# Two of the four weight sums of a pair on GpSimd in block 0, w_out pieces split ahead of the work on h, and a buffer of its own for the first pair

## The chip, the cores and the metric

The kernel runs on one core of a Trainium2 chip. The metric is the time on the device in microseconds (us), the median of several executions.

## The reference, cut to what matters

One layer of a streaming encoder for 2048 prompt frames (x_prompt) and 64 frames of a running stream (x_sample), model width 1024:

```
h = rmsnorm(x) * g_mix
q, f, i, g = split(h @ w_in)               # HGRN2: 8 heads of 128
o = chunked gated recurrence(q, f, i)      # chunks of 64 frames
x = x + (rmsnorm(o) * silu(g)) @ w_out
gate, up = split((rmsnorm(x) * g_ffn) @ w_gu)   # width 2816 each
x = x + (silu(gate) * up) @ w_down
```

Results are also the states of both streams; caches of the layers that this depth does not reach are copied.

## The kernel before, in words

**Blocks.** Frames lie in the free dimension. Block 0 has 576 columns (512 prompt frames and the 64 sample frames, T0), blocks 1 to 3 have 512 (TB). Block 0 is unrolled apart, since `first(b)` is true for it alone; blocks 1 to 3 are one loop. Each block runs through: 8 heads (w_in products with the recurrence of the head before between them), w_out, gate-up with w_gu, and down with w_down, in three groups of 6, 8 and 8 of the 22 gate-up pairs (`GROUPS`), each group followed by its share of down.

**Precision.** Nearly every float32 product is done as three products of split parts: `hi` is a copy rounded to fp32r (ScalarE), `lo` is the rest (VectorE, a subtraction), and TensorE adds hi*hi, hi*lo and lo*hi. So each weight piece of 128x512 costs one ScalarE copy and one VectorE subtraction before TensorE may use it. w_in, w_out and w_down pieces go through a ring of four slots (`w_raw`, `w_hi`, `w_lo`, `LEAD` = 3): L731 is the copy, L910 the subtraction.

**Gate-up.** A pair j is one step of Strassen's method (Winograd's form) over the halves of the 128 gate and 128 up outputs and the two halves of the frames: seven products (`A11, S2, S3, S1, A22, A12, S4`, in this order) of 12 matmuls each (L518 to L520). A11, A12, A22 are raw loads (`g_raw`), S1 to S4 are sums of raw parts (`g_x`): S1 = A21 + A22, S2 = S1 - A11, S3 = A11 - A21, S4 = A12 - S2. In block 0 VectorE makes all four (`weight_sum`, L1121, L1126, L1129, L1134) and SyncE stores S3, S4 and the split parts of S1 and S2 in HBM (`keep`); blocks 1 to 3 load these (`load_kept`). There is one buffer for each operand: while pair j is multiplied, pair j+1 is summed, copied (ScalarE, `gu_high`, L791) and subtracted (VectorE, `gu_low`, L1138), and the raw parts of pair j+2 are loaded as each buffer comes free (`load_first`, `keep`): A21 and A11 once S3 of pair j+1 is summed, then the stores of S3 and, after the subtraction of S1, four stores of S1 and S2, then A22 once its subtraction is done, then S4's store, then A12. All of these are issued by SyncE in this order.

The products are evicted from five banks of PSUM: ScalarE copies A11's to `p1u3` (L817), VectorE adds S2's (`u2`, L1175), S3's (`p1u3`, L1181), and S1's and A22's into `ebuf[:, 0]` (the gate add, L1187), multiplies by the norm `xrstd` (L1192), ScalarE copies A12's (L826), VectorE adds S4's (L1196). S4's product uses A22's bank, so TensorE starts it after the gate add. SiLU (L795), the product with up (L1146), and its split (L799, L1151) give the operand of down.

**Around w_out.** `p1u3` and `u2` are the two halves of `ebuf[:, 1]`, which also holds squares of x for the norm: ScalarE squares a tile into `ebuf[:, 0]` or `[:, 1]` (L615), GpSimd adds it to `ssq` (L1316, eight adds a norm), TensorE sums over partitions with `ones` (`norm_sum`, L291), and ScalarE takes the root (`norm`, L600 to L606). The first pair of a block therefore waits with its first copy (L817) for all eight adds; `norm_sum` stands after the first pair's S4 on TensorE, `norm` behind the copy of A12. `output_group` works off two x tiles at a time: residual add (L1070), scaling (L753), sums and splits of h2 (L1078 to L1095), and between them splits of the next w_out pieces. In blocks 1 to 3 three w_out pieces (6, 7, 8) are split ahead of that work, and piece 9 stands at the end of the first group.

**Last head.** For each head the squares of its output (L643) are split (L651, L988) and summed over partitions (L362, L363), and rstd, scale, y and y's split follow (L657 to L972); TensorE runs products of w_out for the first seven heads in between.

Of the kernel before, what the change touches and what calls it, by code (L numbers as in the profile page):

```python
# [19 lines left out]
P = 128  # L20
EPS = 1e-6
D = 1024
KT = D // P
# [40 lines left out]
def hybrid_layer(nc, x_t, w_all, gain_mix, gain_ffn, bounds, out_gain, state_in, y_t, state_p, state_s,  # L64
# [52 lines left out]
    a_lo, a_end = place("a_lo", [P, GT, T0], F32R)  # L117
    g_at = at[0]
# [148 lines left out]
    p1u3, u2 = ebuf[:, 1, 0:TH0], ebuf[:, 1, TH0:T0]  # L267
# [15 lines left out]
    with nc.Block() as block:  # L283

        @block.tensor
        def _(pe):
# [73 lines left out]
            def out_square_sum(b, h):  # L360
                pe.wait_ge(osq_lo_ready, HEADS * b + h + 1)
                pe.matmul(ps_s[:, 0:TB], ones_r[:], osq_hi[:, 0:TB], start=True, stop=False)  # L362
                mm = pe.matmul(ps_s[:, 0:TB], ones_r[:], osq_lo[:, 0:TB], start=False, stop=True)  # L363
                if first(b):
                    pe.matmul(ps_k[:, 0:CH], ones_r[:], osq_hi[:, TB:T0], start=True, stop=False)
                    mm = pe.matmul(ps_k[:, 0:CH], ones_r[:], osq_lo[:, TB:T0], start=False, stop=True)
                mm.then_inc(oms_done, 1)
# [155 lines left out]
            def gate_up(b, T, j, after_out=False, after_down=None):  # L523

                J = FT * b + j
                if after_out:
# [12 lines left out]
                    for o in (S2, S3, S1, A22, A12):  # L539
                        strassen(b, T, o, KH - 1, KH).then_inc(g_done, 1)  # L540
                    operand_ready(b, j, S4)
                    bank_free(J, S4)
                    strassen(b, T, S4, 0, KH).then_inc(g_done, 1)
                    norm_sum(b, T, 2 * b + 1)
# [53 lines left out]
        def _(act):  # L598
# [41 lines left out]
            def out_squares(b, h):  # L640
# [9 lines left out]
                act.wait_ge(osq_ready, HEADS * b + h + 1)  # L650
                nc.scalar.activation(osq_hi[:, 0:T], osq[:, 0:T], ACT.Copy).then_inc(osq_hi_ready, 1)  # L651
# [149 lines left out]
            def gate_up(b, T, j, j0, more, begun=True, norm_at=None, after_down=None):  # L801

                J, n = FT * b + j, T // 2
                nxt = [o for o in split_of(b)] if more else []
# [10 lines left out]
                if isinstance(j, int) and j == 0:  # L815
                    act.wait_ge(ssq_ready, (KT + 1) * (2 * b + 2))
# [4 lines left out]
                high(S3, S1, A22)  # L821
                act.wait_ge(g_done, OPERANDS * J + A12 + 1)
# [4 lines left out]
                if norm_at is not None:  # L827
                    norm(b, T, norm_at)
# [18 lines left out]
            def block_program(b, T):  # L847
# [57 lines left out]
        def _(dve):  # L905
# [79 lines left out]
            def low_squares(b, h):  # L985
                T = T0 if first(b) else TB
                dve.wait_ge(osq_hi_ready, HEADS * b + h + 1)
                nc.vector.tensor_tensor(osq_lo[:, 0:T], osq[:, 0:T], osq_hi[:, 0:T].bitcast(F32),  # L988
# [109 lines left out]
            def output_group(b, T, i):  # L1098

                def next_piece(u):  # L1100
                    if (i > 0 or u == 3 or first(b)) and (i < KT // 2 - 1 or u == 0):
                        output_pieces(b, i + (u + 3) // 4, (u + 3) % 4, (u + 3) % 4 + 1)
# [13 lines left out]
            def weight_sum(j, o):  # L1116
                if o == S1:
                    dve.wait_ge(g_loaded[RAW_A21], 16 * (j + 1))
                    dve.wait_ge(g_loaded[RAW_A22], 16 * (j + 1))
                    wait(dve, g_lo_ready, OPERANDS * j)  # L1120
                    nc.vector.tensor_tensor(g_x[:, 0], g_raw[:, RAW_A21], g_raw[:, RAW_A22], ALU.add).then_inc(g_sum_ready, 1)  # L1121
                elif o == S2:
                    dve.wait_ge(g_loaded[RAW_A11], 16 * (j + 1))
                    dve.wait_ge(g_sum_ready, 4 * j + 1)
                    wait(dve, g_sum_stored[1], 16 * j)
                    nc.vector.tensor_tensor(g_x[:, 1], g_x[:, 0], g_raw[:, RAW_A11], ALU.subtract).then_inc(g_sum_ready, 1)  # L1126
                elif o == S3:
# [26 lines left out]
            def gate_up(b, T, j, j0, more, begun=True):  # L1154

                J, n = FT * b + j, T // 2
                nxt = list(split_of(b)) if more else []
# [14 lines left out]
                total(S1, S2)  # L1172
# [21 lines left out]
                total(S4)  # L1194
# [4 lines left out]
            def down(b, T, f):  # L1199
                ahead = split_of(b) if f + 1 < len(GROUPS) else ()  # L1200
                last = f + 1 == len(GROUPS)
                for m in range(KT):
# [3 lines left out]
                    if m < len(ahead):  # L1206
                        j1 = GROUPS[f + 1][0]
                        if first(b) and m == 0:
                            for o in (S1, S2, S3):
                                weight_sum(j1, o)  # L1210
# [15 lines left out]
            def block_program(b, T):  # L1226
# [78 lines left out]
        def _(pool):  # L1305
            def sum_squares(nth, T):
# [33 lines left out]
            def block_program(b, T):  # L1340
# [12 lines left out]
                sum_squares(2 * b + 1, T)  # L1353
# [32 lines left out]
        def _(sp):  # L1386
# [98 lines left out]
            def block_program(b, T):  # L1485
# [12 lines left out]
                else:  # L1498
                    sp.wait_ge(y_lo_ready, HEADS * (b + 1))
                    for part in range(3):  # L1500
                        load_kept(b, 0, 0, part)
                        q = OUT0 + (2 + part) * RING
                        load_pieces(b, q, q + RING)
                col = 0 if first(b) else T0 + TB * (b - 1)
                nxt = T0 + TB * b
                for f, (j0, n) in enumerate(GROUPS):
                    with sp.Fori(j0 + 1, j0 + n) as j:
# [3 lines left out]
                    if f < len(GROUPS) - 1:  # L1511
                        load_pieces(b, DN0 + P_GROUP * f + RING, DN0 + P_GROUP * (f + 1) + RING)
# [123 lines left out]
```

## Time and profile before

| | us |
|---|---|
| median of 3 runs | 2716.09 (2714.62 to 2722.4) |
| the profiled execution's own time | 2717.68 |
| its span | 2716.0 |
| TensorE matmul busy | 2607.2 (96%) |
| VectorE busy | 1808.4 (67%) |
| ScalarE busy | 1274.7 (47%) |
| GpSimd busy | 276.2 (10%) |
| mean granted TensorE clock | 0.987 of full |

Engines in the rows: PE is TensorE's matmul, PEld its weight load, DVE VectorE, ACT ScalarE, POOL GpSimd, SP SyncE. "idle before" is the time an engine stood idle ahead of a group of instructions, and "<-" names what ended it. Block 0 takes the first 800 us or so, each other block some 636 us.

### The profile page before, as it was taken

How to read it: one execution, taken by the hardware profiler on the slowest of the kernel's cores; microseconds unless marked ns; L12 is line 12 of the kernel's file. 1: busy time of each engine (PE TensorE's matmuls, PEld its weight loads, DVE VectorE, ACT ScalarE, POOL GpSimd, SP SyncE). 2: the span in 40 equal slices, each digit the busy share in tenths (PEclk: the TensorE clock that was granted, in tenths of full speed). 3: DMA queues.
4: the chain of work that ended last, by engine and by line, in shares of the span. 5: the costliest groups of instructions: out<-in, count | busy, mean ns of one | idle time of the engine just before them, and what ended most of it. 6: DMA issues, size and time to landing. Idle time of an engine off the chain costs nothing.

```text
span 2716.0 us, 53926 instructions
## 1 busy us (share of the span) xinstructions
PE 2607.2 (96%) x16804; PEld 2386.9 (88%) x16804; DVE 1808.4 (67%) x3187; ACT 1274.7 (47%) x2319; POOL 276.2 (10%) x197
## 2 busy tenths in 40 slices
PE   8999979999899999999999999899999999899998
PEld 7999879899898887999997888799898888699897
DVE  6666777876756667676665666767565667767665
ACT  5555543433435555443345555534344555544343
POOL 3111110000011112000002111200002111200001
PEclk9999989999999999999999999999999999999999
DMA  5212335644542223656653222557465222366564
GB/s 183 93 59 62 113 125 165 205 151 143 189 143 71 80 71 105 202 185 194 190 169 107 74 70 82 167 182 240 144 186 160 71 70 74 114 213 211 167 217 147
DMA packets 203414, 379.70 MB, mean 140 GB/s; under 512 B 23168, under 2 KB 23200, under 8 KB 203056
## 3 DMA queue, kind: packets, MB, share of 16 engines
q1 hardware_dynamic: 202896, 369.73, 43.2%
q0 software_dynamic: 384, 8.44, 0.9%
q8 instruction: 53, 0.87, 0.1%
q14 instruction: 81, 0.66, 0.1%
HBM read 331.67 MB, written 52.74 MB: 142 GB/s over the span
## 4 chain that ended last, share of the span: by engine, by line
PE 64%; DVE 4%; issue 3%; ACT 2%; DMA 1%; POOL 1%; SPq 1%; DVEq 0%; ACTq 0%; POOLq 0%
PE ps L426 11%; PE ps L428 11%; PE ps L427 11%; PE ps L518 7%; PE ps L519 7%; PE ps L520 7%; PE ps_s L518 1%; PE ps_s L520 1%; PE ps_s L519 1%; PE ps_u L336 1%; PE ps_s L315 1%; PE ps_o L349 1%; PE ps_u L337 1%; PE ps_o L351 1%; ACT h_raw L753 1%
## 5 line engine op out<-in xcount | busy, mean ns | idle before, releaser
L518 PE MATMUL ps<-h,g_hi 128*128 128x256 f32 (+1 forms) x2112 | 614.7, 291 | 60.1 <-DVE ebuf L1187 34.5
L519 PE MATMUL ps<-h,g_hi 128*128 128x256 f32 (+1 forms) x2112 | 608.9, 288 | 0.0
L520 PE MATMUL ps<-h,g_lo 128*128 128x256 f32 (+1 forms) x2112 | 608.6, 288 | 0.0
L910 DVE TENSOR_TENSOR w_lo<-w_raw,w_hi 128x512 fp32r<-128x512 f32 x512 | 374.5, 733 | 244.9 <-ACT w_hi L731 244.7
L426 PE MATMUL ps<-h_hi,w_hi 128*128 128x512 f32 (+1 forms) x1280 | 472.2, 369 | 16.6 <-DVE h_lo L915 10.1
L731 ACT ACTIVATE w_hi<-w_raw 128x512 fp32r<-128x512 f32 x512 | 318.5, 625 | 330.9 <-PE ps L428 313.9
L518 PEld LDWEIGHTS ps<-h,g_hi 128*128 128x128 f32 x2112 | 406.2, 192 | 69.1 <-DVE ebuf L1187 38.7
L428 PE MATMUL ps<-h_hi,w_lo 128*128 128x512 f32 (+1 forms) x1280 | 452.8, 354 | 0.0
L427 PE MATMUL ps<-h_lo,w_hi 128*128 128x512 f32 (+1 forms) x1280 | 451.2, 352 | 0.0
L426 PE MATMUL ps<-a_hi,w_hi 128*128 128x512 f32 (+1 forms) x1200 | 430.1, 358 | 16.7 <-DVE w_lo L910 13.9
L427 PE MATMUL ps<-a_lo,w_hi 128*128 128x512 f32 (+1 forms) x1200 | 424.4, 354 | 0.0
L428 PE MATMUL ps<-a_hi,w_lo 128*128 128x512 f32 (+1 forms) x1200 | 424.2, 354 | 0.0
L519 PEld LDWEIGHTS ps<-h,g_hi 128*128 128x128 f32 x2112 | 406.0, 192 | 1.2 <-issue 0.7
L520 PEld LDWEIGHTS ps<-h,g_lo 128*128 128x128 f32 x2112 | 405.4, 192 | 0.0
L426 PEld LDWEIGHTS ps<-h_hi,w_hi 128*128 128x128 f32 x1280 | 241.6, 189 | 50.4 <-issue 9.3
L1316 POOL TENSOR_TENSOR ssq<-ssq,ebuf 128x512 f32<-128x512 f32 (+1 forms) x72 | 113.2, 1572 | 1618.5 <-ACT ebuf L615 1617.1
L426 PEld LDWEIGHTS ps<-a_hi,w_hi 128*128 128x128 f32 x1200 | 227.1, 189 | 51.7 <-DVE w_lo L910 16.4
L428 PEld LDWEIGHTS ps<-h_hi,w_lo 128*128 128x128 f32 x1280 | 241.2, 188 | 33.0
L427 PEld LDWEIGHTS ps<-h_lo,w_hi 128*128 128x128 f32 x1280 | 242.0, 189 | 27.1 <-issue 0.7
L791 ACT ACTIVATE g_hi<-g_x 128x512 fp32r<-128x512 f32 x220 | 136.3, 628 | 251.0 <-PE ps L520 120.3
L428 PEld LDWEIGHTS ps<-a_hi,w_lo 128*128 128x128 f32 x1200 | 227.1, 189 | 29.0
L427 PEld LDWEIGHTS ps<-a_lo,w_hi 128*128 128x128 f32 x1200 | 227.3, 189 | 27.4
(160 smaller groups left out, 3819.0 us busy)
## 6 DMA issues: line engine op xcount, KB each, us to landing
w_raw<-w_all SPq DMA_DIRECT2D x516, 256.0 KB, 2.6
g_raw<-w_all SPq DMA_DIRECT2D x286, 256.0 KB, 3.5
g_x<-kept_sum SPq DMA_DIRECT2D x132, 256.0 KB, 3.5
g_hi<-kept_hi SPq DMA_DIRECT2D x132, 256.0 KB, 2.9
g_lo<-kept_lo SPq DMA_DIRECT2D x132, 256.0 KB, 3.2
kept_sum<-g_x SPq DMA_DIRECT2D x44, 256.0 KB, 3.3
kept_hi<-g_hi SPq DMA_DIRECT2D x44, 256.0 KB, 3.2
kept_lo<-g_lo SPq DMA_DIRECT2D x44, 256.0 KB, 3.4
```

What stands on the lines that cost most here:

```text
L315: pe.matmul(ps_s[0:n, 0:n], ke[:, p * P:p * P + n], qe[:, p * P:p * P + n], start=True, stop=True).then_inc(scores_done, 1)
L336: pe.matmul(ps_u[:, 0:P], kx[:, 0, :], v_tok[:, p, :], start=True, stop=True)
L426: pe.matmul(o, w_hi[:, ring, kk, :], hh, start=(k == 0), stop=False)
L427: pe.matmul(o, w_hi[:, ring, kk, :], hl, start=False, stop=False)
L428: last_mm[0] = pe.matmul(o, w_lo[:, ring, kk, :], hh, start=False, stop=stop)
L518: pe.matmul(out, g_hi[:, o, k, :].bitcast(F32R), hh, start=(k == 0 and not more), stop=False, skip_group_check=True)
L519: pe.matmul(out, g_hi[:, o, k, :].bitcast(F32R), hl, start=False, stop=False, skip_group_check=True)
L520: mm = pe.matmul(out, g_lo[:, o, k, :].bitcast(F32R), hh, start=False, stop=last, skip_group_check=True)
L731: nc.scalar.activation(w_hi[:, r, :, :], w_raw[:, r, :, :], ACT.Copy).then_inc(w_hi_ready, 1)
L791: nc.scalar.activation(g_hi[:, o].bitcast(F32R), operand_of(o), ACT.Copy).then_inc(g_hi_ready, 1)
L910: nc.vector.tensor_tensor(w_lo[:, r, :, :], w_raw[:, r, :, :], w_hi[:, r, :, :].bitcast(F32), ALU.subtract).then_inc(w_lo_ready, 1)
L1316: nc.gpsimd.tensor_tensor(ssq[:, 0:T], ssq[:, 0:T], ebuf[:, s, 0:T], ALU.add).then_inc(ssq_ready, 1)
```

## The change

GpSimd makes S1 and S2 of every pair in block 0 (`first_sums`), and VectorE's S3 waits for both. VectorE's S4 sum moves ahead of the gate add. The first pair of each block has `p1u3` and `u2` in `spare` (the last slot of a_lo), so ScalarE's copy no longer waits for `ssq`; the gate add does, and the copy of pair 1 does. `norm_sum` moves ahead of S4 on TensorE, `norm` ahead of A12's copy on ScalarE. In blocks 1 to 3 piece 9 is split with 6 to 8 ahead of the groups, and raw pieces 8 and 9 are loaded before the wait for y. In each block's last head the squares go to TensorE as float32, unsplit. In block 0 the loads for the second pair of a group are issued ahead of down's last four pieces.

```diff
+    spare, _ = place("spare", [P, 2, TH0], offset=a_end - T0 * 4)
-    p1u3, u2 = ebuf[:, 1, 0:TH0], ebuf[:, 1, TH0:T0]
+    def partial(j):
+        two_parts = spare if isinstance(j, int) and j == 0 else ebuf[:, 1].rearrange("p (a n) -> p a n", a=2)
+        return two_parts[:, 0], two_parts[:, 1]
@@ tensor: out_square_sum
+                if isinstance(h, int) and h == HEADS - 1:
+                    pe.wait_ge(osq_ready, HEADS * b + h + 1)
+                    mm = pe.matmul(ps_s[:, 0:TB], ones[:], osq[:, 0:TB], start=True, stop=True)
+                    if first(b):
+                        mm = pe.matmul(ps_k[:, 0:CH], ones[:], osq[:, TB:T0], start=True, stop=True)
+                    mm.then_inc(oms_done, 1)
+                    return
@@ tensor: gate_up, first pair
+                    norm_sum(b, T, 2 * b + 1)
                     operand_ready(b, j, S4)
                     bank_free(J, S4)
                     strassen(b, T, S4, 0, KH).then_inc(g_done, 1)
-                    norm_sum(b, T, 2 * b + 1)
@@ scalar: out_squares
+                if isinstance(h, int) and h == HEADS - 1:
+                    act.sem_inc(osq_hi_ready)
+                    return
@@ scalar and vector: output_group, block_program
-                    if (i > 0 or u == 3 or first(b)) and (i < KT // 2 - 1 or u == 0):
+                    if (i > 0 or first(b)) and (i < KT // 2 - 1 or u == 0):
-                    output_pieces(b, 1, 0, 2)
+                    output_pieces(b, 1, 0, 3)
@@ scalar: gate_up
-                if isinstance(j, int) and j == 0:
+                if isinstance(j, int) and j == 1:
                     act.wait_ge(ssq_ready, (KT + 1) * (2 * b + 2))
 ...
                 high(S3, S1, A22)
+                if norm_at is not None:
+                    norm(b, T, norm_at)
 ...
-                if norm_at is not None:
-                    norm(b, T, norm_at)
@@ vector: low_squares (does nothing for the last head), weight_sum
                 if o == S3:
+                    dve.wait_ge(g_sum_ready, 4 * j + 2)
@@ vector: gate_up
                 low(A11)
-                total(S1, S2)
+                total(S3)
 ...
-                total(S3)
                 low(S3, S1)
+                total(S4)
 ...
+                if isinstance(j, int) and j == 0:
+                    dve.wait_ge(ssq_ready, (KT + 1) * (2 * b + 2))
 ...
                 low(A22, A12)
-                total(S4)
@@ gpsimd
+            def first_sums(j):
+                pool.wait_ge(g_loaded[RAW_A21], 16 * (j + 1))
+                pool.wait_ge(g_loaded[RAW_A22], 16 * (j + 1))
+                wait(pool, g_sum_ready, 4 * j)
+                wait(pool, g_lo_ready, OPERANDS * (j - 1) + S1 + 1)
+                nc.gpsimd.tensor_tensor(g_x[:, 0], g_raw[:, RAW_A21], g_raw[:, RAW_A22], ALU.add).then_inc(g_sum_ready, 1)
+                pool.wait_ge(g_loaded[RAW_A11], 16 * (j + 1))
+                pool.wait_ge(g_sum_ready, 4 * j + 1)
+                wait(pool, g_lo_ready, OPERANDS * j)
+                wait(pool, g_sum_stored[1], 16 * j)
+                nc.gpsimd.tensor_tensor(g_x[:, 1], g_x[:, 0], g_raw[:, RAW_A11], ALU.subtract).then_inc(g_sum_ready, 1)
 ...
+                if first(b):
+                    first_sums(0)
+                    sum_squares(2 * b + 1, T)
+                    with pool.Fori(1, FT) as j:
+                        first_sums(j)
@@ sync
+                    load_pieces(b, OUT0 + 2 * RING, OUT0 + 2 * RING + 2)
                     sp.wait_ge(y_lo_ready, HEADS * (b + 1))
 ...
-                        load_pieces(b, DN0 + P_GROUP * f + RING, DN0 + P_GROUP * (f + 1) + RING)
+                        load_pieces(b, DN0 + P_GROUP * f + RING, DN0 + P_GROUP * (f + 1))
+                        if first(b):
+                            load_pair(b, j0 + n + 1, f + 1)
+                        load_pieces(b, DN0 + P_GROUP * (f + 1), DN0 + P_GROUP * (f + 1) + RING)
```

## Rows read from the trace of the kernel before

**Rows 1.** The page: busy us, share of the span and instructions of each engine.
```profile
PE 2607.2 (96%) x16804; PEld 2386.9 (88%) x16804; DVE 1808.4 (67%) x3187; ACT 1274.7 (47%) x2319; POOL 276.2 (10%) x197
```
**Rows 2.** Waits of TensorE, whole span: us in total, times, longest us.
```profile
PE ps L518 <- DVE ebuf L1187: 34.5, 21, 5.7
PE ps L426 <- DVE w_lo L910: 17.8, 10, 4.4
PE ps L518 <- ACT ebuf L817: 11.7, 3, 3.9
PE ps_s L362 <- DVE osq_lo L988: 5.6, 4, 1.6
```
**Rows 3.** Stretches: length, busy by engine, granted clock, DMA share, GB/s.
```profile
393.13:434.48 41.35, 36.66 (x253) 35.95 (x253) 33.36 (x55) 17.27 (x33) 0.00 (x0) 0.93 0.58 194
495.89:576.65 80.76, 69.92 (x504) 68.51 (x504) 66.58 (x109) 35.13 (x68) 0.00 (x0) 0.98 0.57 196
650.80:736.36 85.56, 74.10 (x504) 72.69 (x504) 66.66 (x109) 35.37 (x68) 0.00 (x0) 0.92 0.54 183
1041.00:1107.00 66.00, 55.35 (x259) 45.87 (x258) 45.26 (x64) 36.14 (x60) 15.17 (x9) 0.90 0.41 128
2313.70:2379.70 66.00, 53.45 (x266) 44.51 (x266) 45.95 (x65) 36.94 (x61) 15.12 (x9) 0.95 0.40 128
```
**Rows 4.** VectorE in order of time, a pair of block 0: start, us.
```profile
534.93 0.75 DVE L1187 TENSOR_TENSOR ebuf<-ps,ebuf 128x576 f32<-128x576 f32 x1
...
536.39 1.29 DVE L1138 TENSOR_TENSOR g_lo<-g_raw,g_hi 128x512 fp32r<-128x512 f32 x2
...
542.28 0.69 DVE L1126 TENSOR_TENSOR g_x<-g_x,g_raw 128x512 f32<-128x512 f32 x1
...
543.82 0.69 DVE L1138 TENSOR_TENSOR g_lo<-g_x,g_hi 128x512 fp32r<-128x512 f32 x1 [0.49 <-ACT g_hi L791]
...
545.58 0.68 DVE L1129 TENSOR_TENSOR g_x<-g_raw 128x512 f32<-128x512 f32 x1
547.04 1.29 DVE L1138 TENSOR_TENSOR g_lo<-g_x,g_hi 128x512 fp32r<-128x512 f32 x2 [0.78 <-ACT g_hi L791]
548.25 0.75 DVE L1187 TENSOR_TENSOR ebuf<-ps,ebuf 128x576 f32<-128x576 f32 x1
```
**Rows 5.** SyncE's issues in the same pair, and raw loads' landing, 508 to 576 us.
```profile
536.52 1.07 SPq L1439 DMA_DIRECT2D kept_lo<-g_lo  x1
537.85 0.57 SPq L1416 DMA_DIRECT2D g_raw<-w_all  x1
DMA to landing us min/median/max: 2.5/3.3/4.1
```
**Rows 6.** GpSimd and VectorE side by side, block 1, in order of time.
```profile
1070.70 1.31 POOL L1316 TENSOR_TENSOR ssq<-ssq,ebuf 128x512 f32<-128x512 f32 x1 [6.20 <-ACT ebuf L615]
1072.64 2.22 POOL L1316 TENSOR_TENSOR ssq<-ssq,ebuf 128x512 f32<-128x512 f32 x1 [0.62 <-ACT ebuf L615]
1073.62 1.78 DVE L910 TENSOR_TENSOR w_lo<-w_raw,w_hi 128x512 fp32r<-128x512 f32 x1
```
**Rows 7.** The ends of blocks 0 and 1, several engines, in order of time.
```profile
361.11 0.35 SPq L1416 DMA_DIRECT2D g_raw<-w_all  x1
...
379.25 0.76 DVE L1192 TENSOR_TENSOR ebuf<-ebuf,xrstd 128x576 f32<-128x576 f32 x1 [6.92 <-ACT xrstd L606]
...
1042.79 0.69 DVE L988 TENSOR_TENSOR osq_lo<-osq,osq_hi 128x512 fp32r<-128x512 f32 x1 [1.62 <-ACT osq_hi L651]
1063.31 1.74 DVE L910 TENSOR_TENSOR w_lo<-w_raw,w_hi 128x512 fp32r<-128x512 f32 x1
1096.11 1.74 DVE L1138 TENSOR_TENSOR g_lo<-g_x,g_hi 128x512 fp32r<-128x512 f32 x1
1097.34 0.38 ACT L817 ACTIVATE ebuf<-ps 128x256 f32<-128x256 f32 x1 [2.05 <-POOL ssq L1316]
1104.66 1.02 PE L291 MATMUL ps_o<-ssq,ones 128*128 128x512 f32 x2
```

More of the change, by code:

```diff
@@ L803, in gate_up @@
                 J, n = FT * b + j, T // 2
+                p1u3, _ = partial(j)
                 nxt = [o for o in split_of(b)] if more else []
@@ L987, in low_squares @@
                 dve.wait_ge(osq_hi_ready, HEADS * b + h + 1)
+                if isinstance(h, int) and h == HEADS - 1:
+                    dve.sem_inc(osq_lo_ready)
+                    return
                 nc.vector.tensor_tensor(osq_lo[:, 0:T], osq[:, 0:T], osq_hi[:, 0:T].bitcast(F32),
@@ L1100, in next_piece @@
                 def next_piece(u):
-                    if (i > 0 or u == 3 or first(b)) and (i < KT // 2 - 1 or u == 0):
+                    if (i > 0 or first(b)) and (i < KT // 2 - 1 or u == 0):
                         output_pieces(b, i + (u + 3) // 4, (u + 3) % 4, (u + 3) % 4 + 1)
@@ L1116, in weight_sum @@
             def weight_sum(j, o):
[L1117 to L1127, printed above, removed]
+                if o == S3:
+                    dve.wait_ge(g_sum_ready, 4 * j + 2)
                     wait(dve, g_sum_stored[0], 16 * j)
@@ L1156, in gate_up @@
                 J, n = FT * b + j, T // 2
+                p1u3, u2 = partial(j)
                 nxt = list(split_of(b)) if more else []
@@ L1208, in down @@
                         if first(b) and m == 0:
-                            for o in (S1, S2, S3):
-                                weight_sum(j1, o)
+                            weight_sum(j1, S3)
                         if first(b) and m == A12:
@@ L1242, in block_program @@
                     output_pieces(b, 0, 3, 4)
-                    output_pieces(b, 1, 0, 2)
+                    output_pieces(b, 1, 0, 3)
                 for i in range(KT // 2):
@@ L1246, in block_program @@
                     if first(b) and i == 1:
-                        for o in (S1, S2, S3):
-                            weight_sum(0, o)
+                        weight_sum(0, S3)
                     if first(b) and i == 3:
@@ L1352, in block_program @@
                     hand_on(carried[3:])
-                sum_squares(2 * b + 1, T)
+                if first(b):
[3 more added lines that the diff above has]
+                        first_sums(j)
+                else:
+                    sum_squares(2 * b + 1, T)
                 sum_squares(2 * b + 2, TB)
@@ L1501, in block_program @@
                         load_kept(b, 0, 0, part)
-                        q = OUT0 + (2 + part) * RING
-                        load_pieces(b, q, q + RING)
+                        q = OUT0 + (2 + part) * RING + 2
+                        load_pieces(b, q, min(q + RING, DN0 + RING))
                 col = 0 if first(b) else T0 + TB * (b - 1)
@@ L1506, in block_program @@
                 for f, (j0, n) in enumerate(GROUPS):
-                    with sp.Fori(j0 + 1, j0 + n) as j:
+                    with sp.Fori(j0 + (2 if first(b) and f > 0 else 1), j0 + n) as j:
                         load_pair(b, j, f)
```

## The prediction

> **What bounds the kernel now.** I read the page first, then TensorE's waits, the granted clock by stretch, one pair of block 0 in order of time, and last the ends of the blocks. TensorE's matmuls are busy 96% of the span [rows 1], so only its holes and the time at the low clock can be won. Its largest waits [rows 2]: 34.5 us in 21 pieces for the gate add (L1187), which is one wait in nearly every pair of block 0; 17.8 for split w_out pieces; 11.7 in three pieces for L817, once in each of blocks 1 to 3; 5.6 in four for L988, once a block. Behind some holes the clock falls to 1.2 from 2.4 GHz: means of 0.93, 0.98 and 0.92 in the three pair loops of block 0 and of 0.90 and 0.95 over two block ends [rows 3]. A stretch at half clock loses half its length, so 66 us at 0.90 lose 6.6 us and at 0.95 3.3.
>
> **The pair loops of block 0.** The stretches of rows 3 run from one S4 product to another: 3, 6 and 6 periods (84 matmuls each) in 41.35 + 80.76 + 85.56 = 207.7 us, 13.8 a pair. An undisturbed period is 548.25 - 534.93 = 13.3 [rows 4]. TensorE alone would need at most 11.7 (69.92 us busy in the second stretch's six periods). VectorE is busy 66.58 of 80.76 us (82%) [rows 3] and carries the cycle. Taking S1 and S2 off it frees 2 x 0.69 = 1.4 us [rows 4], so that a naive sum says 11.9 a pair.
>
> I don't take that, since a second cycle then closes. Call t the end of A22's subtraction (537.05, the first half of the 1.29 at 536.39) [rows 4]. Only then may A22 be loaded for the pair after; only when it lands can GpSimd make S1, then S2; and VectorE's S3, ahead of its eviction of S2's bank, now waits for S2. Step by step:
> - SyncE's issue: today 0.8 us after t (537.85), since the fourth store's issue took 1.07 [rows 5]. A21, A11 and S3's store move 2 us ahead of these stores (S3 is summed sooner), and S4's sum comes between S1's subtraction and t, so SyncE should be free: 0.1. Bounds 0.1 to 0.8.
> - Landing 3.3, bounds 2.5 to 4.1 [rows 5].
> - Two GpSimd sums. The trace has none on these tiles; the nearest rows are its adds on tiles of the same size: 1.31 when VectorE leaves it alone, 2.22 when not [rows 6]. VectorE is idle then, waiting for S2, except for A11's subtraction at the start. So 1.3 each and 0.1 for each of three semaphores: 2.9, bounds 2.9 to 4.7.
> - From S3's start to the end of A22's subtraction: today from S2's sum's end (542.89) to the next A22 subtraction (536.39 + 13.3 = 549.7) are 6.8 us with S3 in them. The waits of 0.49 and 0.78 [rows 4] go, as the copies are ready by then; S4's sum enters (0.6); A22's own subtraction ends it (0.65): 6.8 - 1.3 + 0.6 + 0.65 = 6.75.
>
> Sum: 0.1 + 3.3 + 2.9 + 6.75 = 13.05 a pair, from 12.25 (landing 2.5) to 16.35 (every upper bound). Only 0.25 below today's 13.3: what leaves VectorE comes back as waiting for load and GpSimd. TensorE keeps a hole of some 1.8 us a pair, and I keep 0.35 of the 0.5 that the clock and stray delays add now: 13.4. The first period of the second and third group was 12.6 and 15.0 (in the third S1 and S2 waited for late loads); now the second pair's loads are issued inside down and both sums are made there: 12.0 each. New: 13 x 13.4 + 2 x 12.0 = 198.2, a gain of **9.5** (bounds: 13 x 12.3 + 24 gives 24; 13 x 15 + 26 loses 13).
>
> At issue is whether GpSimd and VectorE disturb each other. Rows 6 show that they do: a GpSimd add beside VectorE's subtraction took 2.22 and the subtraction 1.78, for 1.31 and 0.69 alone. The Trainium skill ("SBUF — State Buffer", Who interferes with whom) says that a VectorE instruction with two SBUF inputs and a GpSimd instruction that reads SBUF exclude each other, whoever starts first holding the port to its end; the trace agrees. By it every sum on GpSimd can hold one subtraction back by its 1.3 us; a VectorE that waits anyway would lose nothing, and the second rival is the case where it doesn't.
>
> **First pair of block 0.** Now `norm_sum` follows S4, and VectorE's multiply at 379.25 waits 6.92 us for xrstd [rows 7], which delays A22's subtraction of pair 1, its whole cycle, and S4 of pair 1, which starts at 393.13, where the first stretch of rows 3 begins. After: GpSimd's sums of pair 1 start when A22 lands (issued at 361.1 [rows 7], + 3.6 = 364.7), S3 at 367.6, the gate add ends 372.9; meanwhile `norm_sum` has run in TensorE's hole and xrstd is there at 373.1, so t is at 374.6 and S4 of pair 1 at 374.6 - 1.35 + 13.0 = 386.2. Gain 393.1 - 386.2 = **6.9** (bounds 3 and 9). S1 and S2 of pair 0 are made on GpSimd before the squares need it; its wait ends with the last tiles, which are bound by TensorE: 0.
>
> **Last head, each block.** The split of the squares goes: copy and subtraction, 0.63 and 0.69 [rows 7], so TensorE's wait, 5.6 us over four blocks [rows 2], goes. A float32 product of 512 columns takes 0.9 to 1.0 (two records from 1104.66, 1.02 [rows 7]) for the two fp32r ones' 0.45: +0.45 on both. Net 1.1 a block, and up to 1.7 more if the 3.4 us of low clock right behind this hole disappear. I take 1.2.
>
> **w_out of blocks 1 to 3.** TensorE waits 3.2 to 4.4 us for piece 9 (most of the 17.8 in rows 2). That wait goes, but VectorE sets the end of this stage: it works nearly without idle time from 1055 to 1098, and TensorE, 3 us earlier, waits for the last two residual tiles instead. What shortens VectorE's own chain is only that piece 9's subtraction, 1.74 beside a GpSimd add [rows 7], is made earlier in 0.6 alone, in the time in which it now waited for a load. Gain 1.1 (bounds 0.3 and 1.7); two raw loads ahead of the wait for y cost nothing, as SyncE only waits there.
>
> **First pair of blocks 1 to 3.** L817 started at 1097.34, 2.05 us after its input, when GpSimd's last add was done [rows 7]. Then A12's first part (1.1), five last parts (1.8), a wait of 0.7, S4 (1.4), `norm_sum` (1.0), 1105.6 in all, part of it at the low clock. After: A12 starts at once, below the wait for the last h2 splits (1096.2); the last parts end at 98.0, `norm_sum` at 98.9, S4 at 100.35; A11 of pair 1 waits for A12's copy, now behind `norm` (table load 1.3, Ln and Exp 1.35): 101.1. Gain 4.5, of which 1.7 is clock that was low from 1098; as the new hole ahead of the last tiles may bring that back, I take 3.5 (bounds 2.5 and 5). S4's operand (1096.11 + 1.74 [rows 7]) is ready before.
>
> A block gives 1.2 + 1.1 + 3.5 = 5.8, three give **17.5** (bounds 9 and 27). Block 0's last head gives **1.2**. Pieces of down that load behind the second pair's loads come about a us before ScalarE wants them: 0, and 1 to 2 each of two times if late.
>
> **Sum.** 9.5 + 6.9 + 17.5 + 1.2 = 35.1 us from the profiled execution's 2717.7 (span 2716.0 and 1.7 around it): 2682.6. The median of the runs is 1.6 below that execution, so 2681 for it; all cases below are given as medians.
>
> **Rivals.**
> 1. The second cycle is shorter than I think: loads land in 2.5, the period falls to 12.3, and with smaller holes the clock stays up at the block ends. 24 + 6.9 + 25 + 1.2 = 57: 2659. For it: today's landings were behind seven transfers in a burst. Against: the median of 3.3 holds for all raw loads. 0.20.
> 2. GpSimd's sums and VectorE's subtractions hold each other up: 15 a pair, loss of 13 for gain of 9.5: 2681 + 22.5 = 2703. For it rows 6; against, VectorE's idle time just there. 0.17.
> 3. The block ends give nearly nothing, as the wait moves to the residual tiles and the clock falls there, and the loops stay at 13.7 a pair: only 6.9 + 1.2 + 3 remain: 2705 to 2715, with luck no change. 0.10.
> 4. **Slower.** The place is VectorE's S3, which waits for GpSimd with everything behind it, the gate add and so TensorE's S4. At 0.8 + 4.1 + 4.7 + 6.75 = 16.35 a pair and the first periods at 15: 13 x 16.35 + 30 = 242.6, a loss of 35 against gains of 25.6, so 2725; it decides from a period of 15.7 on. It needs each upper bound in each pair. 0.05, and 0.03 for another cause of that sign, such as late pieces in down.
>
> **The numbers.** My forecast (2670 to 2697) has 0.45. 0.3% (8 us) is about what a measurement tells from no change: from 2708 to 2724 is the same. Rival 3 splits between faster and same. Faster 0.87, same 0.06, slower 0.07. The range leaves out half of rival 1's far side, part of rival 3 and rival 4: 2656 to 2705.
>
> **What would show it.** S4 to S4 in block 0 near 13.1 to 13.4, VectorE idle 2 to 3 us a pair ahead of L1129 until GpSimd's S2, GpSimd's sums at 1.3 to 1.4 us, A22's load issued within 0.2 us of t: right. Periods under 12.5 or sums over 2 us: wrong. S4 of pair 1 at about 385: right. In blocks 1 to 3 no wait for piece 9, one of 2 to 4 us for L1070 in its place, none for L817, and pair 1 some 6 us earlier. The forecast fails if the wait for L1187 falls below 20 us in all, or if the waits on w_out pieces stay.

## The result, and the profile after

The changed kernel takes 2682.9 us (median of 4, 2681.1 to 2685.4), beside 2716.8 for the kernel before on the same chip (2714.6 to 2722.4). The ratio is 0.9873, 95% interval 0.9856 to 0.9890. The forecast was 2681 in 2656 to 2705. The profiled execution took 2685.4, its span is 2683.7, so the span fell by 32.3 us, for a forecast sum of 35.1.

The page of after, busy us, share and instructions by engine, for [rows 1]:

```profile
PE 2606.4 (97%) x16804; PEld 2386.8 (89%) x16804; DVE 1778.6 (66%) x3139; ACT 1274.2 (47%) x2315; POOL 340.3 (13%) x241
```

TensorE does the same work in the same busy time; VectorE loses 30 us of it and GpSimd gains 64. So what fell is TensorE's idle time. Its waits (us in total, times, longest), for [rows 2]:

```profile
PE ps L529 <- DVE ebuf L1199: 24.5, 17, 2.6
PE ps L529 <- DVE xres L1088: 10.4, 5, 2.8
...
PE ps L437 <- DVE w_lo L925: 9.2, 13, 1.7
```

The gate add (now L1199) still costs one wait in nearly each pair of block 0, 10.0 us less in all. Split w_out pieces fall from 17.8 to 9.2, while the residual tiles rise from 4.4 to 10.4. ScalarE's copy, once 11.7, now shows as 1.9 for its new target, and the wait for the squares' subtraction is gone.

The three stretches of pair loops and the ends of blocks 1 to 3 (length; busy of TensorE, its weight loads, VectorE, ScalarE, GpSimd; granted clock, DMA share, GB/s), for [rows 3]. Each block end is cut from its w_out piece 6 to A11 of pair 1:

```profile
384.86:424.93 40.07, 37.24 (x253) 36.54 (x253) 29.48 (x49) 17.15 (x32) 8.95 (x6) 0.91 0.58 197
485.91:565.48 79.57, 69.93 (x507) 68.52 (x505) 58.23 (x97) 36.07 (x68) 17.48 (x12) 0.98 0.59 197
640.81:720.00 79.19, 69.99 (x507) 68.58 (x505) 57.86 (x97) 36.18 (x68) 17.75 (x13) 0.98 0.57 191
1034.44:1082.22 47.78, 42.78 (x207) 35.41 (x207) 40.76 (x59) 31.52 (x53) 15.49 (x9) 0.93 0.44 139
1663.76:1713.70 49.94, 43.81 (x207) 36.58 (x207) 40.94 (x59) 31.50 (x53) 15.50 (x9) 0.90 0.45 141
2295.34:2345.20 49.86, 43.79 (x206) 36.54 (x207) 40.89 (x59) 31.50 (x53) 15.44 (x9) 0.90 0.46 139
```

The loops take 198.83 instead of 207.67 us, and 6.4 of the 8.8 come from the third. The same three block ends took this long before:

```profile
1053.47:1105.11 51.64, 43.08 (x206) 36.38 (x207) 41.52 (x58) 30.44 (x50) 14.64 (x8) 0.90 0.43 132
1688.79:1741.81 53.02, 43.17 (x206) 36.47 (x207) 41.57 (x58) 30.45 (x50) 14.60 (x8) 0.90 0.43 137
2324.59:2377.02 52.43, 41.98 (x207) 35.38 (x207) 41.58 (x58) 30.45 (x50) 14.59 (x8) 0.93 0.44 139
```

The ledger, from landmarks of both traces (its rounded gains add up to 32.2):

| stretch | before | after | gain | forecast |
|---|---|---|---|---|
| block 0, A11 of pair 0 to S4 of pair 1 | 41.9 | 34.4 | 7.5 | 6.9 |
| block 0, 15 periods of the pair loops | 207.7 | 198.8 | 8.8 | 9.5 |
| block 0, all else | | | 0.0 | 1.2 |
| blocks 1 to 3, head to w_out piece 6 | 757.8 | 753.3 | 4.5 | 3.6 |
| blocks 1 to 3, ends as above | 157.1 | 147.6 | 9.5 | 13.8 |
| all else | | | 1.9 | 0 |

**One pair of block 0.** VectorE of after in order of time (start, us; in brackets idle time before and what ended it), for [rows 4]:

```profile
526.03 1.29 DVE L1147 TENSOR_TENSOR g_lo<-g_raw,g_hi 128x512 fp32r<-128x512 f32 x2
...
529.91 0.69 DVE L1147 TENSOR_TENSOR g_lo<-g_raw,g_hi 128x512 fp32r<-128x512 f32 x1 [0.36 <-ACT g_hi L805]
533.40 0.69 DVE L1138 TENSOR_TENSOR g_x<-g_raw 128x512 f32<-128x512 f32 x1 [2.80 <-POOL g_x L1325]
...
537.81 0.76 DVE L1199 TENSOR_TENSOR ebuf<-ps,ebuf 128x576 f32<-128x576 f32 x1
```

GpSimd's two sums and SyncE's load of A22 in the same pair:

```profile
526.89 0.35 SPq L1443 DMA_DIRECT2D g_raw<-w_all  x1
530.25 1.49 POOL L1320 TENSOR_TENSOR g_x<-g_raw 128x512 f32<-128x512 f32 x1 [10.23 <-DMA g_raw<-w_all]
531.98 1.29 POOL L1325 TENSOR_TENSOR g_x<-g_x,g_raw 128x512 f32<-128x512 f32 x1 [0.24 <-POOL g_x L1320]
```

A22's subtraction ends at t = 526.71. The load is issued 0.18 later (forecast 0.1) and lands at 529.94, after 3.05 (3.3); two sums and their semaphores take until S3 starts at 533.40, 3.46 (2.9); from there to the end of the next A22 subtraction 6.56 (6.75). The sum is 13.25, for a forecast of 13.05 (the 0.35 on top of it in the prediction stood for the clock and stray delays). VectorE is idle for 2.8 us ahead of S3.

All links of the prediction's cycle are there, but the load is not the one that closes it. VectorE's subtraction for A11 begins at 529.91, just ahead of S1, and S1 ends 1.14 behind that subtraction's end at 530.60. Two periods later the load lands 0.2 sooner behind its own t, at 556.61:

```profile
556.76 0.70 DVE L1147 TENSOR_TENSOR g_lo<-g_raw,g_hi 128x512 fp32r<-128x512 f32 x1 [0.35 <-ACT g_hi L805]
556.92 1.68 POOL L1320 TENSOR_TENSOR g_x<-g_raw 128x512 f32<-128x512 f32 x1 [10.01 <-DMA g_raw<-w_all]
```

S1 starts sooner and takes 1.68 instead of 1.49, and again ends 1.14 behind the subtraction. It is so in all eleven pairs of these loops in which S1 begins beside the A11 subtraction: A22 lands 3.01 to 3.32 us behind t, S1 takes between 1.68 and 1.38, and it ends 1.14 to 1.16 behind the subtraction. By the load alone S1 would end at 530.25 + 1.29 = 531.54 and not at 531.74, so the period would be some 13.05 (an estimate from these rows); VectorE's own path is 0.2 longer. The two paths nearly tie.

### The profile page after: what moved, and what is told of

It reads as the page before. It is cut to its first block, busy times and chain, and to the rows that moved or that the text cites. A ratio compares the mean times of both kernels' runs of the same rounds, so it can differ in the third digit from the quotient of the medians.

```text
span 2683.7 us, 54051 instructions
## 1 busy us (share of the span) xinstructions
PE 2606.4 (97%) x16804; PEld 2386.8 (89%) x16804; DVE 1778.6 (66%) x3139; ACT 1274.2 (47%) x2315; POOL 340.3 (13%) x241
## 4 chain that ended last, share of the span: by engine, by line
PE 84%; DVE 6%; issue 4%; ACT 2%; DMA 2%; POOL 1%; DVEq 0%; SPq 0%; POOLq 0%; ACTq 0%
PE ps L437 16%; PE ps L439 15%; PE ps L438 15%; PE ps L529 8%; PE ps L530 8%; PE ps L531 8%; PE ps_s L529 1%; PE ps_s L531 1%; PE ps_s L530 1%; PE ps_u L340 1%; DVE g_lo L1147 1%; PE ps_s L319 1%; DMA g_raw<-w_all 1%; PE ps_o L353 1%; PE ps_u L341 1%
```

## The experiments

Each kernel was timed in several rounds on one chip together with the kernel before, whose median was 2716.8 to 2718.6; kernels are compared by their ratios. "Period" is the mean of the 13 ordinary periods, "usual" their median; "loops" is the 15 periods in all; "ends" are the block ends of blocks 1, 2 and 3 as above. All from the profiled execution but the first two columns.

| kernel | median | ratio (95%) | period, usual | loops | ends |
|---|---|---|---|---|---|
| before | 2716.8 | 1 | 13.86, 13.43 | 207.7 | 51.6 53.0 52.4 |
| after | 2682.9 | 0.9873 (0.9856-0.9890) | 13.30, 13.25 | 198.8 | 47.8 49.9 49.9 |
| e3 sums back | 2693.4 | 0.9902 (0.9877-0.9926) | 13.94, 14.26 | 207.2 | 47.5 48.1 47.1 |
| e2 S1 made twice | 2709.2 | 0.9963 (0.9951-0.9975) | 14.71, 14.63 | 219.8 | 47.9 49.8 47.7 |
| e4 first pair back | 2692.6 | 0.9906 (0.9890-0.9923) | 13.41, 13.25 | 200.2 | 50.1 50.0 50.1 |
| e7 w_out piece back | 2688.7 | 0.9893 (0.9876-0.9909) | 13.26, 13.25 | 198.3 | 49.7 49.5 51.5 |
| e6 squares split | 2684.7 | 0.9881 (0.9861-0.9900) | 13.26, 13.25 | 198.2 | 48.1 47.4 48.1 |
| e5 loads after down | 2682.6 | 0.9870 (0.9850-0.9889) | 13.27, 13.24 | 198.9 | 47.4 47.3 47.4 |
| e1 eviction first | 2673.6 | 0.9838 (0.9815-0.9862) | 12.96, 13.17 | 192.9 | 47.3 47.3 47.1 |
| e8 e1, S4's sum late | 2673.3 | 0.9835 (0.9814-0.9856) | 12.82, 12.92 | 190.7 | 47.1 47.1 47.1 |
| e9 e1, A22 early | 2667.9 | 0.9822 (0.9805-0.9838) | 12.56, 12.54 | 187.4 | 48.1 47.1 48.1 |
| e10 load before stores | 2702.8 | 0.9941 (0.9925-0.9958) | 14.48, 14.50 | 216.7 | 47.9 47.3 48.1 |
| e12 both before stores | 2679.6 | 0.9861 (0.9841-0.9882) | 13.26, 13.24 | 198.3 | 47.6 47.5 47.2 |
| e11 e9, S4's store too | 2662.6 | 0.9797 (0.9774-0.9820) | 12.01, 12.00 | 179.5 | 47.1 47.6 49.8 |

**e3: S1 and S2 back on VectorE.**

```diff
-                if o == S3:
-                    dve.wait_ge(g_sum_ready, 4 * j + 2)
+                if o == S1: ... nc.vector.tensor_tensor(g_x[:, 0], g_raw[:, RAW_A21], g_raw[:, RAW_A22], ALU.add)
+                elif o == S2: ... nc.vector.tensor_tensor(g_x[:, 1], g_x[:, 0], g_raw[:, RAW_A11], ALU.subtract)
-                total(S3)
+                total(S1, S2)
...
+                total(S3)
                 low(S3, S1)
-                total(S4)
...
                 low(A22, A12)
+                total(S4)
```

> The changed kernel with S1 and S2 back on VectorE, in the order of the kernel before (S4's sum after the subtraction of A12 again); all else as changed. Theory (moving the sums won 0.1 to 0.5 us a pair and the first periods of the groups): the loops cost 7 to 10 us more than in the changed kernel, so 2690 to 2693; S4 to S4 13.3 with low-clock stretches between. Rival (the sums were worth nothing and the loops gained by the load order and a clock that fell less): 2681 to 2685.

Measured: loops 207.2, so the move of the sums is worth 8.4 us there, and the stretch from A11 of pair 0 to S4 of pair 1 takes 3.3 longer too (37.75). By the ratios e3 is 8 us slower than after, which the two intervals only just tell apart, since its block ends, which the edit doesn't touch, came out 4.9 shorter. Its usual periods come in two sorts, 13.2 to 13.4 and 14.26 to 14.28, and the first sort is as short as the 13.25 of after. What each sort holds, in three kernels (columns as above; each line is one period, from S4 to S4). Before:

```profile
549.05:562.42 13.37, 11.43 (x84) 11.19 (x85) 11.12 (x19) 5.72 (x11) 0.00 (x0) 1.00 0.58 192
562.42:576.65 14.23, 12.88 (x84) 12.64 (x84) 11.20 (x19) 5.83 (x11) 0.00 (x0) 0.88 0.55 191
```

e3:

```profile
547.85:561.03 13.18, 11.42 (x84) 11.19 (x85) 11.11 (x19) 5.71 (x11) 0.00 (x0) 1.00 0.58 203
561.03:575.31 14.28, 12.97 (x85) 12.73 (x85) 11.20 (x19) 5.83 (x11) 0.00 (x0) 0.88 0.55 186
```

After:

```profile
525.37:538.62 13.25, 11.43 (x85) 11.20 (x85) 9.69 (x17) 5.84 (x11) 2.78 (x2) 1.00 0.61 201
538.62:552.26 13.64, 12.96 (x84) 12.72 (x85) 10.12 (x17) 5.66 (x11) 3.15 (x2) 0.87 0.56 192
```

A period with a stretch of 3.4 us at 1.2 GHz in it (0.87 or 0.88 on its mean) costs 0.9 to 1.1 us in the first two kernels and 0.4 in after; in e5 one such period of 13.26 stands beside 13.24 at full clock. Two periods of before and one of e3 have a longer stretch (0.81 or 0.82) and take 15.15 to 15.37. VectorE shows why. In the slow period of before and in that of after:

```profile
565.71 0.46 DVE L1196 TENSOR_TENSOR fbuf<-ps,ebuf 128x288 f32<-128x288 f32 x1 [0.74 <-PE ps L520]
```

```profile
541.79 0.46 DVE L1207 TENSOR_TENSOR fbuf<-ps,ebuf 128x288 f32<-128x288 f32 x1 [1.23 <-PE ps L531]
547.04 0.69 DVE L1138 TENSOR_TENSOR g_x<-g_raw 128x512 f32<-128x512 f32 x1 [1.27 <-POOL g_x L1325]
```

TensorE, at half clock right behind its hole, makes VectorE wait in both. Before, S1 and S2 follow at once on VectorE and all is later by that. After, VectorE would wait 2.80 for GpSimd anyway, and waits 1.27 instead: most of the delay is absorbed. In this period S1 had begun before the late A11 subtraction, so it isn't held by it. Of 13 ordinary periods before had five with such stretches, at 14.2 to 15.4; after has four, at 13.24 to 13.64. Over the undisturbed 13.3 of before its periods lose 7.2 us in all, and over its 13.25 after's lose 0.7. So of the 8.8 us of the loops 6.5 are this, 1.6 are the first periods of groups 2 and 3, and 0.7 is the shorter cycle. Before's five stretches are also longer, 23.9 us in all for 13.7 in after's four; why is not shown.

**e2: S1 made twice on GpSimd**, with a semaphore between.

```diff
+                nc.gpsimd.tensor_tensor(g_x[:, 0], g_raw[:, RAW_A21], g_raw[:, RAW_A22], ALU.add).then_inc(sum_twice, 1)
+                pool.wait_ge(sum_twice, j + 1)
```

> The changed kernel with S1 made twice in a row on GpSimd in every pair of block 0 (the same value written again). Theory (GpSimd's sums are a link of the cycle): each period grows by the added instruction and its semaphore, about 1.5 us, from 13.25 to 14.7; 15 periods and the first pair give 20 to 24 us, so about 2705. Rival (VectorE's or TensorE's own work sets the period and GpSimd's sums lie beside it): no change, 2680 to 2685.

Measured: by the ratios 24 us slower than after; the period grows by 1.41, near the 1.5 expected, and VectorE's S3 waits 1.4 longer (2.80 in after):

```profile
533.27 0.69 DVE L1139 TENSOR_TENSOR g_x<-g_raw 128x512 f32<-128x512 f32 x1 [4.17 <-POOL g_x L1328]
```

GpSimd is a link of the cycle with its full length, as the second cycle of the prediction has it; an engine at 13% of the span sets the pace of this stage.

**e4, e7, e6, e5: one other part undone in each.**

```diff
# e4: ScalarE's copy into ebuf again, norm_sum behind S4, norm behind A12's copy
-                if isinstance(j, int) and j == 1:
+                if isinstance(j, int) and j == 0:
                     act.wait_ge(ssq_ready, (KT + 1) * (2 * b + 2))
# e7: piece 9 split in its group, raw pieces 8 and 9 loaded behind the wait for y
-                    output_pieces(b, 1, 0, 3)
+                    output_pieces(b, 1, 0, 2)
# e6: the last head's squares split again
-                if isinstance(h, int) and h == HEADS - 1: ...
# e5: the second pair's loads behind down's last four pieces
-                    with sp.Fori(j0 + (2 if first(b) and f > 0 else 1), j0 + n) as j:
+                    with sp.Fori(j0 + 1, j0 + n) as j:
```

> The changed kernel with the first pair's part undone in all blocks: p1u3 and u2 in the square buffer again, ScalarE's first copy waits for all eight adds, norm_sum after S4 and norm after A12's copy. Theory (prediction: 6.9 us in block 0 and 3.5 in each other): 17 us slower than the changed kernel, near 2700, with a wait of 4 us for the copy back in blocks 1 to 3. Rival (TensorE would wait for the residual tiles and h2 parts anyway, so this part won less): 2686 to 2692.

> The changed kernel with the w_out part undone: piece 9 at the end of the first group again, its raw loads behind the wait for y. Theory (VectorE sets the end of this stage, TensorE only waits in another place): TensorE waits 3.2 to 4.4 us for piece 9 again in each of blocks 1 to 3, the wait for the last residual tiles (2.85 in the changed kernel) shrinks, and the cost is 1 us a block, 2685 to 2687 in all. Rival (the wait for piece 9 was time on the path): 3.5 a block, 2692 to 2694.

> The changed kernel with the last head's squares split into hi and lo again. Theory (prediction): the wait of 1.3 to 1.6 us for the subtraction is back in each block, 1.1 us a block from the squares to the last y product, 4 to 5 us in all, 2686 to 2688. Rival (the float32 product costs TensorE as much as the split did): 2682 to 2684.

> The changed kernel with the loads of the second pair of groups two and three behind down's last pieces again. Theory: in these two places GpSimd's sums start 1 to 3 us later, so 1 to 5 us in all, 2684 to 2688. Rival: these loads land before the group begins anyway, no change.

Measured, by the ratios: e4 is 9 us slower than after (17 expected), e7 5 and e6 2 (both within what the intervals leave open, so that they rest on the traces), e5 the same. In e4 block 0's first pair takes 4.8 longer (A11 of pair 0 to S4 of pair 1 39.25), and each block end is 50.0. For the block ends after is a poor yardstick, since two of its three were at a lower clock than in most others. e12, which differs from after only in block 0, has them so:

```profile
1035.00:1082.59 47.59, 42.68 (x206) 35.24 (x206) 40.72 (x59) 31.50 (x53) 15.50 (x9) 0.93 0.43 138
1663.28:1710.80 47.52, 41.59 (x206) 34.28 (x207) 40.74 (x59) 31.52 (x53) 15.50 (x9) 0.96 0.42 139
```

In block 2 both wait 3.8 us in two pieces for the residual tiles; the clock is 0.96 here and 0.90 in after, which is worth 0.06 x 48 = 2.9 us, and 2.4 is all that lies between them. From 47.3, the usual length in the other kernels, the first pair undone costs 2.8 a block (3.5 expected; part of it is the clock, 0.90 in e4's ends) and the w_out part 2.3 (e7's first two; its third, 51.5, has more time at the low clock), between the 1 expected and the 3.5 of its rival; both undone, as before, cost 4.3 to 5.7. In e7 TensorE's wait for split w_out pieces is back at 18.5 us and that for the residual tiles falls to 5.6:

```profile
PE ps L437 <- DVE w_lo L925: 18.5, 10, 4.5
...
PE ps L529 <- DVE xres L1088: 5.6, 6, 1.0
```

So the wait for piece 9 did move to the residual tiles, and only part of it was won. e6 loses 0.6 a block on the mean of its head stretches (251.7 for 251.1), less than forecast, and e5 nothing.

**e1 and e8: S2's bank evicted ahead of S3.** In block 0 the u2 add and what follows it run before VectorE waits for GpSimd; e8 puts S4's sum back behind A22's and A12's subtractions too.

```diff
-                total(S3)
...
-                low(S2)
+                if not first(b):
+                    low(S2)
...
+                if first(b):
+                    total(S3)
+                    low(S2)
```

> The changed kernel with VectorE's evictions of the S2 and S3 products and the subtraction for a_lo moved ahead of the S3 sum in block 0 (ScalarE's copy for a_hi ahead of S2's copy), so that they lie in the 2.8 us in which VectorE waits for GpSimd's S2. Theory (cycle: A22's load, two GpSimd sums, S3, and VectorE's work down to A22's subtraction; 13.25 us a pair in the changed kernel): the part behind S3 shrinks by about 1.2 us, so S4 to S4 is 12.0 to 12.1 in the loops of block 0 and the time is 14 to 17 us below the changed kernel's, near 2667. Rival (the total of VectorE's or SyncE's work, or the port shared with GpSimd, sets the period): the same instructions in another order, so 13.2 and 2680 to 2685. Second rival (moved evictions now collide with GpSimd's sums): sums over 2 us each and no gain or a loss.

> e1_evict_first with VectorE's S4 sum behind the subtraction of A12 again, as in the kernel before. Theory: the cycle loses another 0.6 us, 11.4 to 11.6 a pair, which is close to TensorE's own 11.2, so 6 to 9 us below e1_evict_first, near 2659. Rival (by then another link, S4's store before GpSimd's S2 or the gate add, holds): no further gain.

Measured: both 9 to 10 us faster than after. For e1 that falls short of the 14 to 17 expected, its mean period is 12.96 for 12.0 to 12.1. VectorE waits between nothing and 1.88 for GpSimd instead of 2.80, and part of what left the chain behind S3 came back ahead of it. GpSimd in one pair:

```profile
503.20 1.91 POOL L1323 TENSOR_TENSOR g_x<-g_raw 128x512 f32<-128x512 f32 x1 [9.58 <-DVE g_lo L1147]
505.34 1.30 POOL L1328 TENSOR_TENSOR g_x<-g_x,g_raw 128x512 f32<-128x512 f32 x1 [0.24 <-POOL g_x L1323]
```

S1 takes 1.91 beside VectorE's a_lo subtraction for 1.3 alone, and A22's load, issued behind the fourth store at 499.18, landed after 3.7 for 3.05. e8's loops are 2.2 us shorter in the profile, but its time is e1's, and not the 6 to 9 us less that were expected.

**e10: A22's load ahead of the four stores, nothing else.**

```diff
+                if nxt is not None:
+                    sp.wait_ge(g_lo_ready, OPERANDS * j + A22 + 1)
+                    load_raw(nxt, RAW_A22, f)
                 sp.wait_ge(g_lo_ready, OPERANDS * j + S1 + 1)
                 for o in PAIRED: ...
```

> The changed kernel with A22's load ahead of the four stores of S1 and S2 in SyncE's order, nothing else. Theory (the landing of A22 is a link of the cycle): it lands 2.6 instead of 3.1 us after its issue and S1 starts that much sooner: periods of 12.7 instead of 13.25, 7 to 9 us off the time, about 2675. Rival (landing is hidden behind something else): 2681 to 2685. If the stores now delay S4's store and GpSimd's S2, which waits for it, the gain is smaller.

Measured: some 19 us slower than after. The expectation, 7 to 9 us faster, was wrong; it had named S4's store only as something that would make the gain smaller. GpSimd of e10 in one pair:

```profile
510.55 1.71 POOL L1320 TENSOR_TENSOR g_x<-g_raw 128x512 f32<-128x512 f32 x1 [9.92 <-DMA g_raw<-w_all]
513.84 1.29 POOL L1325 TENSOR_TENSOR g_x<-g_x,g_raw 128x512 f32<-128x512 f32 x1 [1.58 <-DMA kept_sum<-g_x]
```

S2's buffer is also S4's, and S2 may be made only when S4's store has left it. That store is issued behind the load and the stores, which moved it 1.6 us past GpSimd's need.

**e9, e11, e12: the same store as a wait.** e9 is e1 with A22's subtraction right behind the gate add and its load ahead of the stores. e11 moves S4's store ahead of the four others too. e12 does both moves of SyncE in after.

```diff
+                if first(b):
+                    low(A22)
                 # SyncE, e11: S4's store, then
+                sp.wait_ge(g_lo_ready, OPERANDS * j + S1 + 1)
+                for o in PAIRED: ... the four stores
```

> e1_evict_first, with A22's subtraction made right after the gate add in block 0 and A22's load issued by SyncE ahead of the four stores of S1 and S2. In e1_evict_first the 1.3 us taken out behind S3 came back ahead of it: A22's load landed 3.7 us after its issue behind the four stores (3.1 in the changed kernel), and GpSimd's S1 took 1.9 beside VectorE's subtraction. Theory (cycle through load, sums and S3): load 2.6, sums 3.1, S3 to A22's subtraction 4.0 with the semaphores are some 9.8, under TensorE's own 11.2, so TensorE sets the pace: S4 to S4 at 11.3 to 11.7, nearly no wait for the gate add, and 2653 to 2660. Rival (VectorE's work with the port shared with GpSimd sets the period): 12.4 to 12.8 a pair as in e1_evict_first, so 2670.

> e9_a22_early with S4's store issued right after A22's load, so ahead of the four stores of S1 and S2. In e9_a22_early GpSimd's S2 waited 1.6 us for S4's store (both use one buffer), which had moved behind those four. Theory: the wait goes, S2 follows S1 at once, and the period falls from 12.4 to TensorE's own: 11.3 to 11.5, with the waits for the gate add under 5 us in all; 12 to 15 us below e9_a22_early, 2653 to 2656. Rival (VectorE and the shared port limit at 12.4): 2667.

> The changed kernel with A22's load and S4's store ahead of the four stores in SyncE's order, nothing else. e10_load_before_stores, which moved the load alone, was 19 us slower than the changed kernel, as S4's store had come to lie behind the four stores and GpSimd's S2 waited for it. Theory: with S4's store ahead as well, A22 lands sooner and nothing else is late: 12.7 to 12.9 a pair (13.25 in the changed kernel), 2674 to 2678. Rival (the order of these transfers costs by itself): 2683 or more.

Measured: all three gained less than expected. e9's period is 12.56 for 11.3 to 11.7, with the same wait of 1.57 in front of S2. In e11 that wait is gone and the period is 12.0, for 11.3 to 11.5:

```profile
510.40 1.51 POOL L1327 TENSOR_TENSOR g_x<-g_raw 128x512 f32<-128x512 f32 x1 [8.80 <-DMA g_raw<-w_all]
512.15 1.46 POOL L1332 TENSOR_TENSOR g_x<-g_x,g_raw 128x512 f32<-128x512 f32 x1 [0.24 <-POOL g_x L1327]
```

TensorE's waits for the gate add between 380 and 760 us fall from 24.3 in after to 9.9. e11 is the fastest kernel of the study, 0.8% under after and 2.0% under before. What limits it is VectorE itself: in five periods it is busy 55.20 of 60.06 us, waits 3.7 for ScalarE's copies and never for GpSimd, and its instructions beside GpSimd's sums take longer, as in the pair above:

```profile
511.10 1.36 DVE L1147 TENSOR_TENSOR g_lo<-g_raw,g_hi 128x512 fp32r<-128x512 f32 x1 [0.35 <-ACT g_hi L805]
512.75 1.47 DVE L1160 TENSOR_TENSOR a_lo<-fbuf,a_hi 128x576 f32 x1
```

Alone they take 0.69 and 0.75. That is the mechanism of the rival that was named for e11, at 12.0 instead of 12.4.

e12 is no faster in its period (13.26, for 12.7 to 12.9 expected): freed of the store, the cycle is closed elsewhere. VectorE and GpSimd of e12 in one pair, for the same three instructions of after above:

```profile
530.83 0.69 DVE L1147 TENSOR_TENSOR g_lo<-g_raw,g_hi 128x512 fp32r<-128x512 f32 x1 [0.36 <-ACT g_hi L805]
...
534.33 0.69 DVE L1138 TENSOR_TENSOR g_x<-g_raw 128x512 f32<-128x512 f32 x1 [2.80 <-POOL g_x L1325]
```

```profile
531.11 1.56 POOL L1320 TENSOR_TENSOR g_x<-g_raw 128x512 f32<-128x512 f32 x1 [10.15 <-DMA g_raw<-w_all]
```

S1 begins earlier, but takes 1.56 (1.76 in another pair) instead of 1.49 and ends 1.15 us behind the end of VectorE's A11 subtraction: 531.52 to 532.67 here, 530.60 to 531.74 in after. The edit moved the landing little, from 3.01 to 3.32 behind t in after to 2.86 to 3.19 here, but even this small gain went nowhere. A load that lands sooner only makes S1 longer, as between the pairs of after. That S1 is held by that subtraction fits both traces and the durations of [rows 6]; no kernel here took the subtraction away to show it.

## Why the prediction was right, point by point

- **Bound and naive sum.** Right: TensorE's busy time did not change, and the gain is its holes. 11.9 a pair, from VectorE's busy time alone, was rightly refused; it took e11's moves to come to 12.0.
- **The pair loops.** 8.8 for 9.5. That a second cycle closes through GpSimd's two sums is right, and e2 shows it. One step of it failed: A22's load is not on it. VectorE's subtraction for A11, which the prediction had named and priced at nothing, holds S1 until 1.14 us behind its end, and that path is 0.2 longer than the one through the load (above). So 13.25 came for 13.05, and the sum is as near as it is because the two paths nearly tie. The clock's term is mis-sized. The prediction put the gain of an ordinary pair at 0.25 for the cycle and 0.15 for the clock (0.35 of 0.5 kept). The cycle gave 0.05 (13.25 for 13.3), and what disturbed periods add fell from 0.55 a pair to 0.05. Here the step that failed is "a stretch at half clock loses half its length". In a stage that VectorE paces it loses what VectorE can't make good: for a stretch of 3.4 us 0.9 to 1.1 before and 0 to 0.4 after, where half the length is 1.7.
- **First periods of groups 2 and 3.** 12.96 each for 12.0. Before had 12.63 and 14.90. The early loads aren't needed for the third: e5 has 12.95 there without them (in the second it has 13.44, with a stretch at the low clock). Nor are GpSimd's sums: e3, with the early loads, has 12.90 there with VectorE's. Either may be enough; no kernel undid both. The sum of both is 1.6 for a forecast of 3.6, the one term in the loops that fell short.
- **GpSimd and VectorE disturbing each other (rival 2).** S1 takes 1.49 and S2 1.29; the prediction took 1.3 each, and the bound of 2.22 [rows 6] did not come. (The add of 1.31 in rows 6, read there as left alone by VectorE, had a subtraction beside it from 0.07 us after its start, which took 1.79: the one that began first kept its time.) The Trainium skill ("SBUF — State Buffer", Who interferes with whom) has both exclude each other to the end of the one that holds the port. The trace agrees: only the sum that begins beside a subtraction is longer, and it ends 1.14 to 1.16 behind the subtraction, whenever it began. It costs the 0.2 a pair above and not 1.3, as VectorE then waits for that sum.
- **First pair of block 0.** 7.5 for 6.9; e4 gives 4.8 of it back and e3 3.3, so part of it is the sums' move. The multiply by xrstd waits 1.42 for 6.92 us, and S4 of pair 1 starts at 384.86 (386.2).
- **Last head.** In block 0 the hole went as forecast, from the product of the outputs to the last y product in 7.9 us for 9.0. But a stretch of 3.4 us at 1.2 GHz, which before does not have, begins at 310.1 right behind it, and at A11 of pair 0 only 0.2 of the 1.1 is left (49.6 us from the same product for 49.8). Blocks 1 to 3 gave 2.7, 1.5 and 0.4; e6 shows 0.6 a block, so what the first has over that isn't this edit's own.
- **w_out and the first pair of blocks 1 to 3.** Forecast 4.6 a block, measured 3.9, 3.1 and 2.6; e12, with more of them at full clock, has 4.1, 5.5 and 5.2. The mechanisms are right: no wait for L817's old target, residual tiles late by 2.8 in place of piece 9. What failed is the clock's share: I had kept 0.7 of the 1.7, and the three ends have 27.3 us at 1.2 GHz, as many as before, so that it gave back nothing. In two of them the stretch behind the new hole lasts 10.2 us (3.4 in e12), which cost about 2.5 each. The clock's share is 2.1 of the 4.3 us that these ends fall short; which of the two edits lacks the rest is not shown.
- **Rivals.** Rival 1 (landing in 2.5, clock up at the block ends) failed on both halves, with landings of 3.05 and 0.90 to 0.93 at the block ends; rival 3 on both, as the loops came to 13.3 and the block ends gave 9.5. Rival 4 needed a period of 15.7; even with one sum made twice it is 14.7, and the kernel stayed faster than before.

Short of the forecast are the loops by 0.7, the rest of block 0 with its last head by 1.2, and the block ends by 4.3; over it the first pair by 0.6, the other heads by 0.9 and what I had at nothing by 1.9. The 2.8 us of the whole are what these leave of each other, so the total is more right than its terms.

## What to carry to other kernels

When work moves to an idle engine, draw the cycles it closes (load, sum, wait, eviction, next load; and the pacing engine's own work that the sums run beside) and price their links, not the busy time saved: here 1.4 us off VectorE shortened the undisturbed cycle by 0.05. A wait that the new cycle puts on the pacing engine can still be worth having, as it takes up delays of others. And before a transfer is moved forward in a queue, look up for each one it passes whose buffer waits for it: one load ahead of four stores cost 19 us, and with one store moved along as well, nothing.

## What the runs showed that was not expected

- A stretch of TensorE at 1.2 GHz costs a stage between nothing and a third of its length, by where the pacing engine has slack: 13.24 and 13.26 a period at a mean of 1.00 and 0.87 in e5, 13.18 and 14.28 at 1.00 and 0.88 in e3.
- The same block end, the same instructions and the same two waits of 2.8 and 1.0 us, ran at a mean clock of 0.90 in after and 0.96 in e12, 49.9 and 47.5 us (block 2). Only the work some 900 us earlier differs, so a difference of 2 us in such a stretch says nothing of an edit.
- SyncE's issue of a 256 KB transfer takes 0.35 us for the first store of a burst and 1.13 for the fourth in e1; in after that fourth takes 0.40 to 0.73 in the pairs shown by its trace from 524 to 540 us.
